# One-hot tables outside the sixth weight slot in a one-core MoE layer: the slot is loaded ahead of them, ScalarE scales their token half, and shared products run in another order

## The chip, the cores and the metric

The kernel runs on one core of one Trainium2 chip. The metric is the device time of one execution in microseconds (us). The profiled execution is a separate run whose span, from the first to the last instruction, is a little shorter than its own device time.

## What is computed

One layer of a hybrid decoder for 512 prompt tokens and 8 sample tokens (520 in all), width 1024, everything in float32. A token mixer (one input projection to seven parts, a short gated convolution, a Conformer convolution module, a gated merge and an output projection) is followed by a mixture of experts with 64 experts of width 256, of which each token takes 8, and one shared expert. The part that the change touches:

```python
m = sigmoid(g_a) * y_a + sigmoid(g_b) * y_b
x = x + gt1 * rmsnorm(m @ w_o, g_post1)
h = rmsnorm(x, g_pre2) * (1 + sc2) + sh2
scores = sigmoid(h @ w_router)             # 64 experts in 8 groups
# best 4 groups, then the 8 best experts of a token -> gate
act    = silu(h @ w1[e]) * (h @ w3[e]) * gate
routed = sum over e of act @ w2[e]
shared = (silu(h @ ws1) * (h @ ws3)) @ ws2
x = x + gt2 * rmsnorm(routed + shared, g_post2)
```

## The kernel before

Each engine has an instruction list written out by hand, and semaphores order the lists. An engine runs its own list strictly in order, so a wait holds up everything behind it. SP issues nearly all loads, ACT (ScalarE) issues the writes of small results, POOL (GpSimd) issues the gathers and scatters of token rows.

**The projection w_o.** Weights are split into a rounded part and a remainder, so that three fast products give the accuracy of float32. ACT makes the rounded part, POOL subtracts it from the loaded block in `raw` to get the remainder, 128 by 1024 elements at a time (L569 and L618). Items 72 to 79 are the eight column blocks of w_o, and their parts are kept in `w_kept`. TensorE (PE) uses them in `half_product(u)`, 24 matmuls for each u, once for tokens 0 to 255 and once for the others (L1746, L1747, L1750). The remainder of item 73 is written where the merged activations' remainder `m_lo` and others were needed before, so POOL waits at n = 73 until VectorE (DVE) has made the last piece of `m_lo` (L1247), and then serves items 73, 74 and so on. SP reloads a `raw` buffer once the remainder of its last item is there.

**Norm, residual, router.** After the sixteen half products PE, ACT and DVE alternate over x1, h2 and the router's logits. ACT copies x1 and h2, turned into token rows, out of PSUM and writes them to DRAM (`x1_dram`, semaphore `spill`; `h2_rows`, L1006 and L1008, semaphores `rows_out`). Token tile i has 128 tokens, and tile 4 has the last 8. DVE then picks the experts and gives every (token, expert) pair a place in a list of strips of 64 rows. There are at most 66 jobs of two strips (`JOBS`).

**The one-hot stage.** To turn places into row lists, DVE makes four arrays for each token tile: `oneEs` (job number equal, L1367, 528 half floats a partition), `oneA` (row number equal, L1368, 1024), and the two halves of `oneB`: `oneEs` times the token's number (L1370) and `oneEs` times the choice's number (L1371). PE multiplies them (L1856, 8 matmuls a tile, all summed in one bank). All five tiles' arrays lie side by side in the sixth weight slot, `act5[:, 2 * R + SLOT:...]`. PE then spreads the result (`idx_pe`, L1867), DVE makes the gather indices `idxG` (L1389), the run tables (`table_dve`) and a row of last passes (`early_dve` 1, L1408), and POOL issues the gather of pass 0 into `scr` and of pass 1 into `conv` (L645).

**The shared expert** is 16 + 16 + 32 matmuls of `shared_up(f, m, half)` (L1787) that PE runs wherever it would otherwise wait. ACT takes Silu (`shared_gate`) and a copy (`shared_value`), and POOL multiplies the two (`shared_gated`, L623).

**The expert loop.** Six weight slots of 3 MB each (w1, w3 and w2 of an expert). Experts 0 to 3 go to slots 1 to 4, expert 4 to slot 5 (the sixth), expert 5 to slot 0, and from expert 6 on a slot is refilled by SP (`refill`, L380 and L385) when PE has done its last pass with it. A pass takes two strips of 64 rows: DVE turns the gathered rows into `xe` (`rows_T`, L1444, two halves), PE makes the up products (L1882), DVE and ACT the activation, PE the down products (L1896), ACT copies out, and POOL scatters. The slots share memory with h2: the sixth lies where the one-hot arrays are and after them, `xe` lies over three of the eight blocks of `hT` that `shared_up` reads.

Of the kernel before, what the change touches and what calls it, by code (L numbers as in the profile page):

```python
# [7 lines left out]
F16 = mybir.dt.float16  # L8
I32 = mybir.dt.int32
U32 = mybir.dt.uint32  # L10
ALU = mybir.AluOpType
# [4 lines left out]
P = 128  # L16
# [6 lines left out]
def build_program(  # L23
# [33 lines left out]
    with ctx:  # L57
# [151 lines left out]
        one_of = act5[:, 2 * R + SLOT:2 * R + 2 * SLOT]  # L209
        NA, NB = TOPK * P // 2, TOPK * JOBS  # L210
        oneA = one_of[:, 0:TT * NA].bitcast(F16).rearrange("p (i k n r) -> p i k n r", i=TT, k=TOPK // 2, r=2)
        oneB = one_of[:, TT * NA:TT * (NA + NB)].bitcast(F16).rearrange("p (i k a n r) -> p i k a n r", i=TT, k=TOPK // 2, a=2, r=2)
        oneEs = [t.rearrange("p k e -> p (k e)")[:, 0:NB // 2].bitcast(F16).rearrange("p (k n r) -> p k n r", k=TOPK // 2, r=2) for t in (eq, eqm)]
        assert TT * (NA + NB) <= SLOT
# [18 lines left out]
        def s8(n):  # L233
# [47 lines left out]
                 "m_hi_dve aff_act gp_pe gm_dve early_dve early_pe last_pass_dve x1t_T x1t_done x1t_dve h2_dve oneE_dve sh_mm sh_ev sh_act "  # L281
# [49 lines left out]
        def _(sp):  # L331
# [56 lines left out]
            for k in range(3 * C):  # L388
                w = (w_out_a, w_out_b, w_o)[k // C]
                sp.wait_ge(S["w_lo"], 56 + k + (1 if k < 4 else 4))  # L390
# [4 lines left out]
            sp.wait_ge(S["w_lo"], 80 + NU)  # L395
# [12 lines left out]
            up_weights(1, 2, ((w1, 0),))  # L408
            sp.wait_ge(rows_out[0], 16 * 3)
# [4 lines left out]
            up_weights(4, 5)  # L414
            down_weights(4, 5)
# [94 lines left out]
        def _(pool):  # L510
# [102 lines left out]
            for n in range(72, 80):  # L613
                hi, lo = w_kept[n - 72]
                if n == 73:
                    pool.wait_ge(S["m_lo_dve"], C)
                pool.wait_ge(S["w_hi"], n + 1)
                pool.tensor_tensor(lo, raw[(n - 56) % 4], hi, ALU.subtract).then_inc(S["w_lo"], 1)  # L618
# [5 lines left out]

            shared_gated(0)
# [87 lines left out]
        def _(act):  # L713
# [283 lines left out]
            hx_at = [hx[:, 0, :], hx[:, 1, :], conv[:, 0:D], sflat[:, 0:D]]  # L997

            def h2_rows_out(i):
                n, t = (P if i < TT - 1 else LAST), hx_at[i % 4]  # L1000
                act.wait_ge(S["hx_T"], i + 1)
                if i == 2:
                    act.wait_ge(g2_out, 16)
                elif i == 4:
                    act.wait_ge(rows_out[0], 16 * 2)
# [23 lines left out]

            shared_value(0)  # L1030
            h2_rows_out(4)
            shared_gate(1)
# [42 lines left out]
        def _(dve):  # L1075
# [172 lines left out]

            dve.wait_ge(S["tailrows_act"], 1)
# [109 lines left out]
            def numbers(n):  # L1359
                return iot[:, 0:n, :].unsqueeze(1).to_broadcast([P, TOPK // 2, n, 2])  # L1360
# [4 lines left out]
            dve.wait_ge(spill, 16 * TT)  # L1365
            for i in range(TT):
                tt(oneEs[i % 2], numbers(JOBS), pairs_of(job_of[:, i], JOBS), ALU.is_equal).then_inc(S["oneE_dve"], 1)  # L1367
                tt(oneA[:, i], numbers(P), pairs_of(row_of[:, i], P), ALU.is_equal).then_inc(S["oneE_dve"], 1)  # L1368
                dve.wait_ge(S["oneE_dve"], 2 * i + 1)
                ts(oneB[:, i, :, 0], oneEs[i % 2], tokp1[:, i:i + 1], None, ALU.mult)  # L1370
                tt(oneB[:, i, :, 1], oneEs[i % 2], pairs_of(kv[:, i, :].rearrange("p (k r) -> p k r", r=2), JOBS), ALU.mult  # L1371
                   ).then_inc(S["idx_ab"], 1)
# [5 lines left out]
            dve.wait_ge(S["idx_mm"], 1)  # L1378
# [67 lines left out]

            dve.wait_ge(S["es_pe"], 2)
# [3 lines left out]
            dve.wait_ge(S["sh_mm"], 2 * FT)  # L1451
            for h in range(2):
                rows_T(0, 64, h)
# [53 lines left out]
        def _(pe):  # L1507
# [224 lines left out]
            def half_product(u):  # L1732

                a, b = part["AB"[u // C]]
                hi, lo = w_kept[item[u]]
                out = ps[:, u % 3, 0:b - a]
                if u < C:
                    pe.wait_ge(S["w_lo"], 72 + u + NU + 1)
# [12 lines left out]
                ins.then_inc(items_used, 1)  # L1751
# [28 lines left out]
            def shared_up(f, m, h, k0=0, k1=C):  # L1780
# [5 lines left out]
                for k in range(k0, k1):  # L1786
                    ins = mm(ps[:, bank, at:at + b - a], w[:, k, :], hT[:, k, a:b], start=(k == 0), stop=(k == C - 1))  # L1787
                if h == "B" and k1 == C:
                    ins.then_inc(S["sh_mm"], 1)

# [61 lines left out]
            shared_up(1, 0, "A")  # L1852
            for i in range(TT):
                pe.wait_ge(S["idx_ab"], i + 1)
                for k in range(TOPK):
                    ins = mm(ps[:, 7, 0:2 * JOBS], oneA[:, i, k // 2, :, k % 2],  # L1856
                             oneB[:, i, k // 2, :, :, k % 2].rearrange("p a n -> p (a n)"), start=(i == 0 and k == 0),
                             stop=(i == TT - 1 and k == TOPK - 1))
            ins.then_inc(S["idx_mm"], 1)
# [11 lines left out]
            shared_up(1, 1, "A")  # L1871
            pe.wait_ge(S["sh_ev"], 1)
            shared_up(1, 0, "B")
            pe.wait_ge(S["sh_ev"], 2)
            shared_up(1, 1, "B")
# [24 lines left out]
            pe.wait_ge(S["early_dve"], 1)  # L1900
            mm(ps[0:1, 6, P:P + 1 + TT], red[0:1 + TT, 2:3], ident[0:1 + TT, 0:1 + TT], start=True, stop=True).then_inc(S["es_pe"], 1)
# [140 lines left out]
```

## Time and profile before

| what | value |
|---|---|
| time, median of 3 runs | 1235.48 us (1234.01 to 1235.58) |
| the profiled execution's own time | 1235.82 us |
| its span | 1234.10 us |
| busy: PE, DVE, POOL, ACT | 95%, 46%, 42%, 26% |
| mean granted TensorE clock | 0.983 of full speed |
| read and written in DRAM | 322.21 MB and 33.30 MB |

How to read it: busy shares are taken over the whole span, and the stages differ. Up to about 500 us the projections run, to 557 us the w_o products, to 615 us norm, router, one-hot stage and the rest of the shared expert, and from there to 1196 us the expert loop. A granted clock of 1.00 is 2.4 GHz and 0.50 is 1.2 GHz.

### The profile page before, as it was taken

How to read it: one execution, taken by the hardware profiler on the slowest of the kernel's cores; microseconds unless marked ns; L12 is line 12 of the kernel's file. 1: busy time of each engine (PE TensorE's matmuls, PEld its weight loads, DVE VectorE, ACT ScalarE, POOL GpSimd, SP SyncE). 2: the span in 40 equal slices, each digit the busy share in tenths (PEclk: the TensorE clock that was granted, in tenths of full speed). 3: DMA queues.
4: the chain of work that ended last, by engine and by line, in shares of the span. 5: the costliest groups of instructions: out<-in, count | busy, mean ns of one | idle time of the engine just before them, and what ended most of it. 6: DMA issues, size and time to landing. Idle time of an engine off the chain costs nothing.

```text
span 1234.1 us, 26531 instructions
## 1 busy us (share of the span) xinstructions
PE 1167.9 (95%) x9397; PEld 847.9 (69%) x9398; DVE 563.0 (46%) x956; ACT 325.8 (26%) x633; POOL 514.3 (42%) x522
## 2 busy tenths in 40 slices
PE   4899999999999899999899999997989999899997
PEld 3599999999999899897755555544545554455542
DVE  4285676658568868337643322221112222222234
ACT  3522322323323451435121121111111111111122
POOL 2144444445448343600355444542344455344420
PEclk9899999999999899999999999998999999999999
DMA  9954345435421233548399999999999999999887
GB/s 307 324 177 147 86 146 166 140 91 160 151 81 41 69 85 101 143 168 338 127 405 410 401 397 412 411 414 415 413 411 413 411 413 399 411 415 410 342 319 267
DMA packets 149035, 337.48 MB, mean 273 GB/s; under 512 B 14807, under 2 KB 99363, under 8 KB 123369
## 3 DMA queue, kind: packets, MB, share of 16 engines
q1 hardware_dynamic: 129304, 296.57, 64.0%
q0 software_dynamic: 16656, 34.14, 7.3%
q10 hardware_dynamic: 3025, 6.07, 1.4%
q8 instruction: 35, 0.57, 0.2%
q14 instruction: 15, 0.12, 0.0%
HBM read 322.21 MB, written 33.30 MB: 288 GB/s over the span
## 4 chain that ended last, share of the span: by engine, by line
PE 74%; DMA 13%; issue 5%; DVE 4%; POOL 2%; SPq 1%; ACT 0%; DVEq 0%; POOLq 0%; ACTq 0%
PE ps L1882 23%; DMA w<-in_w_dram 10%; PE ps L1896 10%; PE ps L1602 9%; PE ps L1603 9%; PE ps L1604 9%; DMA ring<-in_w_ada_dram 2%; PE ps L1890 2%; PE ps L1746 1%; PE ps L1955 1%; PE ps L1615 1%; PE ps L1747 1%; PE ps L1750 1%; PE ps L1988 1%; PE ps L1544 1%
## 5 line engine op out<-in xcount | busy, mean ns | idle before, releaser
L1882 PE MATMUL ps<-w,xe 128*64 (+1 forms) x3136 | 378.2, 393 | 21.1 <-DMA w<-in_w_dram 19.2
L1882 PEld LDWEIGHTS ps<-w,xe 128*64 128x64 f32 x3136 | 221.6, 136 | 171.7 <-issue 55.8
L569 POOL TENSOR_TENSOR wsplit<-ring,wsplit 128x1024 fp32r<-128x1024 f32 x72 | 175.3, 2435 | 252.2 <-ACT wsplit L721 222.1
L1602 PE MATMUL ps<-h_s_hi,wsplit 128*128 128x260 f32 x960 | 272.3, 284 | 0.0
L1604 PE MATMUL ps<-h_s_hi,wsplit 128*128 128x260 f32 x960 | 270.8, 282 | 0.0
L1603 PE MATMUL ps<-h_lo_m_hi,wsplit 128*128 128x260 f32 x832 | 234.9, 282 | 0.0
L1464 DVE TENSOR_TENSOR rs<-sg,ps 128x128 f32<-128x128 f32 x98 | 28.2, 288 | 365.5 <-ACT sg L1051 365.5
L1602 PEld LDWEIGHTS ps<-h_s_hi,wsplit 128*128 128x128 f32 x960 | 180.8, 188 | 6.7 <-issue 5.9
L1896 PE MATMUL ps<-w,eactT 128*64 128x512 f32 (+1 forms) x784 | 184.8, 592 | 0.0
L1604 PEld LDWEIGHTS ps<-h_s_hi,wsplit 128*128 128x128 f32 x960 | 180.9, 188 | 0.0
L1603 PEld LDWEIGHTS ps<-h_lo_m_hi,wsplit 128*128 128x128 f32 x832 | 156.7, 188 | 0.0
L1164 DVE SCALAR_TENSOR_TENSOR ps<-conv,vecs,ps 128x512 f32<-128x512 f32 x224 | 154.7, 746 | 0.0
L721 ACT ACTIVATE wsplit<-ring 128x1024 fp32r<-128x1024 f32 x74 | 78.5, 1061 | 274.0 <-PE ps L1604 267.3
L645 POOL DMA_INDIRECT scr<-h_rows,gidx x100 | 102.1, 1021 | 42.8 <-issue 22.9
L645 POOL DMA_INDIRECT conv<-h_rows,gidx x100 | 101.3, 1013 | 44.4 <-issue 24.6
L1896 PEld LDWEIGHTS ps<-w,eactT 128*64 128x64 f32 x784 | 54.3, 136 | 64.4 <-issue 53.6
L640 POOL COPY gidx<-tail 128x4 int32 (+1 forms) x50 | 10.5, 210 | 188.3 <-DVE xe L1444 180.0
L1039 ACT ACTIVATE act<-ps 128x1024 f32<-128x1024 f32 x50 | 51.2, 1024 | 117.5 <-PE ps L1896 112.6
L1051 ACT ACTIVATE sg<-ps 128x128 f32<-128x128 f32 x98 | 27.1, 277 | 190.8 <-PE ps L1882 190.8
L1053 ACT ACTIVATE eactT<-ps 128x128 f32<-128x128 f32 x98 | 27.2, 277 | 172.2 <-PE ps L1890 172.2
L1444 DVE STREAM_TRANSPOSE xe<-conv 128x512 f32<-128x512 f32 x50 | 56.2, 1123 | 33.8 <-PE ps L1882 30.2
L1444 DVE STREAM_TRANSPOSE xe<-scr 128x512 f32<-128x512 f32 x50 | 55.9, 1119 | 31.3 <-PE ps L1882 31.3
(357 smaller groups left out, 1373.0 us busy)
## 6 DMA issues: line engine op xcount, KB each, us to landing
w<-in_w_dram SPq DMA_DIRECT2D x192, 1024.0 KB, 21.6
ring<-in_w_in_dram SPq DMA_DIRECT2D x56, 512.0 KB, 3.8
ring<-in_w_ada_dram SPq DMA_DIRECT2D x8, 2048.0 KB, 8.8
ring<-in_w_ada_dram SPq DMA_DIRECT2D x8, 1024.0 KB, 26.5
ring<-y_rows SPq DMA_DIRECT2D x4, 2048.0 KB, 18.2
ring<-in_w_out_a_dram SPq DMA_DIRECT2D x8, 512.0 KB, 3.6
ring<-in_w_out_b_dram SPq DMA_DIRECT2D x8, 512.0 KB, 3.5
ring<-in_w_o_dram SPq DMA_DIRECT2D x8, 512.0 KB, 3.7
```

The costliest lines, as they stand in the source:

```text
L569: pool.tensor_tensor(wsplit[:, b, 1], raw[raw_slot], wsplit[:, b, 0], ALU.subtract).then_inc(S["w_lo"], 1)
L645: pool.indirect_dma_start(out=xgs[u][:, g * QR:(g + 1) * QR], out_offset=None, in_=h2_rows.rearrange("t (q d) -> (t q) d", q=4), in_offset ...
L721: act.activation(wsplit[:, b, 0], raw[raw_slot], ACT.Copy).then_inc(S["w_hi"], 1)
L1039: act.activation(yb[:, 1 - u, :], ps[:, 4:6, :].rearrange("p b n -> p (b n)"), ACT.Copy).then_inc(S["ex_yd"], 1)
L1164: chain(stt(out=acc[k % 2] if k != KC - 2 else cvj, in0=glu[:, k:k + NP], scalar=vecs[:, ds(j + (V_WC + 8 * k), 1)], in1=acc[k % 2], op0=A ...
L1444: dve.transpose(out=xe[:, 4 * h:4 * h + 4, :].rearrange("p k (g s) -> p g k s", g=4), in_=xgs[u].rearrange("p (g r k) -> p g k r", g=4, k= ...
L1464: tt(eact[:, cols], esil[:, cols], ps[:, 2 + f, P:2 * P], ALU.mult).then_inc(S["ex_mul"], 1)
L1602: mm(ps[:, bank + h, 0:HT], wsplit[:, b, 0, k, :], hi[:, k, p:q], start=(k == 0), stop=False)
L1603: mm(ps[:, bank + h, 0:HT], wsplit[:, b, 0, k, :], lo[:, k, p:q], start=False, stop=False)
L1604: ins = mm(ps[:, bank + h, 0:HT], wsplit[:, b, 1, k, :], hi[:, k, p:q], start=False, stop=(k == C - 1))
L1882: ins = mm(ps[a * STRIP:(a + 1) * STRIP, 2 + f, 0:2 * P], xe[:, k, a * STRIP:(a + 1) * STRIP], w[a][:, f, k], start=(k == 0), stop=(k == C ...
L1896: ins = mm(ps[a * STRIP:(a + 1) * STRIP, 4 + h, :], eactT[:, k, a * STRIP:(a + 1) * STRIP], w[a][:, k, h * 512:(h + 1) * 512], start=(k == ...
```

## The change

1. **Item 73.** DVE, right after the last piece of `m_lo`, subtracts item 73 itself. POOL skips it and waits for DVE before item 74. PE's second half product waits for DVE. SP's block k = 21 waits for DVE too, and the other counts of `w_lo` go down by one.
2. **One-hot buffers.** The arrays of tile i lie in one of two buffers, in `conv` and in `scr`. DVE and ACT wait for PE's use of a buffer two tiles back. The h2 rows of tiles 2 and 3, which lay there, go through the two `hx` buffers, with waits for the writes of two tiles back.
3. **The sixth slot.** Expert 4 is loaded by SP as soon as the x1 rows are written. It was loaded after the one-hot products and the first gather.
4. **Token half.** ACT makes the token half of `oneB` for each tile (`token(i)`), in its list between the h2 copies and around `shared_value(0)`.
5. **Shared products.** `shared_up(1, 0, "A")` is cut into four pairs of steps between the tiles' products. The first three steps of the remaining three products (those that read what `xe` covers) come first, then the small product L1901 that follows `early_dve` 1, then the other fifteen steps. DVE's first `rows_T` waits for the nine steps only and stands ahead of the table step for `early_dve` 2, for which PE waits before it enters the expert loop.
6. **POOL** waits for the last one-hot product before `shared_gated(0)`.

```diff
+        ones_at = [conv[:, 0:NA + NB], sflat[:, 0:NA + NB]]
...
-            sp.wait_ge(S["idx_mm"], 1)
-            sp.wait_ge(xg_in[0], 64)
+            sp.wait_ge(spill, 16 * TT)
             up_weights(4, 5)
             down_weights(4, 5)
+            sp.wait_ge(rows_out[0], 16 * 3)
+            sp.wait_ge(rows_out[1], 16 * 2)
+            down_weights(5, 0)
...
+            pool.wait_ge(S["idx_mm"], TT)
             shared_gated(0)
...
+            def token(i):
+
+                act.wait_ge(S["oneE_dve"], 2 * i + 1)
+                if i >= 2:
+                    act.wait_ge(S["idx_mm"], i - 1)
+                act.activation(oneB[i % 2][:, :, 0], oneEs[i % 2], ACT.Copy, scale=tokp1[:, i:i + 1]).then_inc(S["token_act"], 1)
+
+            token(0)
+            token(1)
             shared_value(0)
             h2_rows_out(4)
+            for i in range(2, TT):
+                token(i)
...
+            dve.wait_ge(S["w_hi"], 74)
+            tt(w_kept[1][1], raw[1], w_kept[1][0], ALU.subtract).then_inc(S["m_lo_dve"], 1)
...
             for i in range(TT):
+                if i >= 2:
+                    dve.wait_ge(S["token_act"], i - 1)
                 tt(oneEs[i % 2], numbers(JOBS), ...)
+                if i >= 2:
+                    dve.wait_ge(S["idx_mm"], i - 1)
+                tt(oneA[i % 2], numbers(P), ...)
-                ts(oneB[:, i, :, 0], oneEs[i % 2], tokp1[:, i:i + 1], None, ALU.mult)
+                tt(oneB[i % 2][:, :, 1], oneEs[i % 2], ...).then_inc(S["idx_ab"], 1)
...
+            dve.wait_ge(S["h2_read"], 1)
+            for h in range(2):
+                rows_T(0, 64, h)
             dve.wait_ge(S["es_pe"], 2)
             link(ts(last_pass, ps[0:1, 6, P:P + 1 + TT], 4.0 * P - 1.0, None, ALU.add), "early_dve")
...
+                ins.then_inc(S["idx_mm"], 1)
+                if i < TT - 1:
+                    shared_up(1, 0, "A", 2 * i, 2 * i + 2)
...
+            turn = (1, 2, 3, 0, 4, 5, 6, 7)
+            shared_up(1, 1, "A", 0, 3, turn)
+            pe.wait_ge(S["sh_ev"], 2)
+            shared_up(1, 0, "B", 0, 3, turn)
+            shared_up(1, 1, "B", 0, 3, turn).then_inc(S["h2_read"], 1)
+            pe.wait_ge(S["early_dve"], 1)
+            mm(ps[0:1, 6, P:P + 1 + TT], ...).then_inc(S["es_pe"], 1)
+            shared_up(1, 1, "A", 3, C, turn)
+            shared_up(1, 0, "B", 3, C, turn)
+            shared_up(1, 1, "B", 3, C, turn)
```

## Rows read from the trace of the kernel before

**Rows 1.** Waits of PE from 600 us on: total us, times, longest us.

```profile
PE ps L1882 <- DMA w<-in_w_dram: 19.2, 6, 6.2
PE ps L1856 <- DVE act L1371: 1.1, 2, 0.9
```

**Rows 2.** Timeline of PE: start, duration, line, tiles, count, idle before.

```profile
603.21 10.84 PE L1787 MATMUL ps<-act,ring 128*128 128x256 f32 x48
...
615.92 6.57 PE L1882 MATMUL ps<-w,xe 128*64 x56 [1.76 <-DVE xe L1444]
...
627.58 6.51 PE L1882 MATMUL ps<-w,xe 128*64 x56
...
638.76 6.53 PE L1882 MATMUL ps<-w,xe 128*64 x56
```

**Rows 3.** Windows: each engine's busy time, then granted clock, DMA share, GB/s.

```profile
586.00:588.00 2.00, 2.00 (x28) 1.68 (x26) 1.00 (x6) 0.36 (x2) 0.00 (x0) 1.00 0.23 88
...
616.00:618.00 2.00, 2.00 (x18) 1.31 (x20) 2.00 (x2) 0.00 (x0) 1.98 (x3) 1.00 0.99 414
...
700.00:705.00 5.00, 5.00 (x42) 2.37 (x40) 3.34 (x5) 0.83 (x3) 1.42 (x2) 1.00 0.86 329
...
760.00:780.00 20.00, 20.00 (x164) 11.21 (x162) 4.17 (x6) 3.71 (x8) 10.94 (x14) 1.00 1.02 415
```

**Rows 4.** Timeline around item 73.

```profile
502.23 2.41 POOL L618 TENSOR_TENSOR wsplit<-ring,wsplit 128x1024 fp32r<-128x1024 f32 x1 [5.71 <-DVE m_lo L1247]
502.47 2.26 DVE L1252 SCALAR_TENSOR_TENSOR s<-ada,vecs 128x72 f32<-128x72 f32 x1
...
504.69 0.39 PE L1746 MATMUL ps<-h_lo_m_hi,wsplit 128*128 128x256 f32 x1 [2.10 <-POOL wsplit L618]
```

**Rows 5.** A window of 1 us, and two steps of the chain that ended last.

```profile
506.00:507.00 1.00, 1.00 (x7) 1.00 (x6) 0.00 (x0) 0.00 (x0) 1.00 (x2) 0.50 0.86 259
...
509.58 0.32 PE ps L1746
...
512.86 0.32 PE ps L1746
```

**Rows 6.** Groups of DVE by form: count, then total us and mean ns.

```profile
L1504 DVE TENSOR_TENSOR act<-act,ring 128x1024 f32<-128x1024 f32 x4 | 4.9, 1225 | 0.1
```

**Rows 7.** Timeline of DVE in the one-hot stage, tiles 0 and 1.

```profile
592.51 0.43 DVE L1367 TENSOR_TENSOR act<-iot,act 128x528 f16<-128x528 f16 x1
...
593.47 0.35 DVE L1370 TENSOR_SCALAR act<-act,tokp 128x528 f16<-128x528 f16 x1
...
595.02 1.38 DVE L1370 TENSOR_SCALAR act<-act,tokp 128x528 f16<-128x528 f16 x1
```

**Rows 8.** Timeline of PE in the one-hot stage.

```profile
594.64 3.62 PE L1787 MATMUL ps<-act,ring 128*128 128x256 f32 x16
598.10 1.59 PE L1856 MATMUL ps<-act 128*128 128x132 f16 x24
```

**Rows 9.** Timeline of ACT and POOL in the one-hot stage.

```profile
594.25 0.39 ACT L1022 ACTIVATE rs<-ps 128x264 f32<-128x264 f32 x1
...
594.71 1.54 POOL L623 TENSOR_TENSOR scr<-sg,rs 128x520 f32<-128x520 f32 x1 [71.94 <-ACT rs L1022]
594.84 1.01 ACT L1006 ACTIVATE ring<-ps 8x1024 f32<-8x1024 f32 x1 [0.21 <-PE ps L1831]
```

**Rows 10.** Timeline of DVE from the index products to pass 1.

```profile
602.51 0.17 DVE L1382 TENSOR_SCALAR table<-act 1x64 int32<-1x64 f32 x1
...
603.44 0.69 DVE L1389 TENSOR_SCALAR tail<-ps,red 128x264 int32<-128x264 f32 x1
...
614.52 2.07 DVE L1444 STREAM_TRANSPOSE xe<-scr 128x512 f32<-128x512 f32 x2
```

**Rows 11.** Timeline of SP's queue: the loads of expert 4's w1 and w3.

```profile
612.66 0.80 SPq L380 DMA_DIRECT2D w<-in_w_dram  x2
```

**Rows 12.** The chain of work that ended last, a step at 847 us.

```profile
847.29 0.50 issue
```

More of the change, by code:

```diff
@@ L208, in build_program @@
         sflat = scr[:, :, :].rearrange("p n t -> p (n t)")
-        one_of = act5[:, 2 * R + SLOT:2 * R + 2 * SLOT]
         NA, NB = TOPK * P // 2, TOPK * JOBS
-        oneA = one_of[:, 0:TT * NA].bitcast(F16).rearrange("p (i k n r) -> p i k n r", i=TT, k=TOPK // 2, r=2)
-        oneB = one_of[:, TT * NA:TT * (NA + NB)].bitcast(F16).rearrange("p (i k a n r) -> p i k a n r", i=TT, k=TOPK // 2, a=2, r=2)
+        ones_at = [conv[:, 0:NA + NB], sflat[:, 0:NA + NB]]
+        assert NA + NB <= min(sum(wide_n), 4 * T)
+        oneA = [t[:, 0:NA].bitcast(F16).rearrange("p (k n r) -> p k n r", k=TOPK // 2, r=2) for t in ones_at]
+        oneB = [t[:, NA:NA + NB].bitcast(F16).rearrange("p (k a n r) -> p k a n r", k=TOPK // 2, a=2, r=2) for t in ones_at]
         oneEs = [t.rearrange("p k e -> p (k e)")[:, 0:NB // 2].bitcast(F16).rearrange("p (k n r) -> p k n r", k=TOPK // 2, r=2) for t in (eq, eqm)]
-        assert TT * (NA + NB) <= SLOT
         QR = D // 4
@@ L408, in _ @@
             up_weights(1, 2, ((w1, 0),))
+            sp.wait_ge(spill, 16 * TT)
+            up_weights(4, 5)
+            down_weights(4, 5)
             sp.wait_ge(rows_out[0], 16 * 3)
@@ L615, in _ @@
                 if n == 73:
-                    pool.wait_ge(S["m_lo_dve"], C)
+                    continue
+                if n == 74:
+                    pool.wait_ge(S["m_lo_dve"], C + 1)
                 pool.wait_ge(S["w_hi"], n + 1)
@@ L1778, in logits, with shared_up @@
                 mark(ins, "logits_pe")
-            def shared_up(f, m, h, k0=0, k1=C):
+            def shared_up(f, m, h, k0=0, k1=C, turn=tuple(range(C))):
                 w = ws13[:, m].rearrange("p (k n) -> p k n", k=C)[:, :, f * P:(f + 1) * P]
@@ L1785, in shared_up @@
                 bank = 3 - 3 * f if h == "A" else 1 + m
-                for k in range(k0, k1):
-                    ins = mm(ps[:, bank, at:at + b - a], w[:, k, :], hT[:, k, a:b], start=(k == 0), stop=(k == C - 1))
+                for n in range(k0, k1):
+                    k = turn[n]
+                    ins = mm(ps[:, bank, at:at + b - a], w[:, k, :], hT[:, k, a:b], start=(n == 0), stop=(n == C - 1))
                 if h == "B" and k1 == C:
                     ins.then_inc(S["sh_mm"], 1)
+                return ins
             pe.wait_ge(S["t_cp"], 16)
@@ L1851, in _ @@
             h2_T(4)
-            shared_up(1, 0, "A")
             for i in range(TT):
                 pe.wait_ge(S["idx_ab"], i + 1)
+                pe.wait_ge(S["token_act"], i + 1)
                 for k in range(TOPK):
-                    ins = mm(ps[:, 7, 0:2 * JOBS], oneA[:, i, k // 2, :, k % 2],
-                             oneB[:, i, k // 2, :, :, k % 2].rearrange("p a n -> p (a n)"), start=(i == 0 and k == 0),
+                    ins = mm(ps[:, 7, 0:2 * JOBS], oneA[i % 2][:, k // 2, :, k % 2],
+                             oneB[i % 2][:, k // 2, :, :, k % 2].rearrange("p a n -> p (a n)"), start=(i == 0 and k == 0),
                              stop=(i == TT - 1 and k == TOPK - 1))
-            ins.then_inc(S["idx_mm"], 1)
+                ins.then_inc(S["idx_mm"], 1)
+                if i < TT - 1:
+                    shared_up(1, 0, "A", 2 * i, 2 * i + 2)
             pe.wait_ge(S["es_dve"], 1)
@@ L1869, in _ @@
             mark(ins, "idx_pe")
-            shared_up(1, 1, "A")
-            pe.wait_ge(S["sh_ev"], 1)
-            shared_up(1, 0, "B")
+            turn = (1, 2, 3, 0, 4, 5, 6, 7)
+            assert R + D >= R + T and R + 2 * D <= R + 4 * T
+            shared_up(1, 1, "A", 0, 3, turn)
             pe.wait_ge(S["sh_ev"], 2)
-            shared_up(1, 1, "B")
+            shared_up(1, 0, "B", 0, 3, turn)
+            shared_up(1, 1, "B", 0, 3, turn).then_inc(S["h2_read"], 1)
+            pe.wait_ge(S["early_dve"], 1)
+            mm(ps[0:1, 6, P:P + 1 + TT], red[0:1 + TT, 2:3], ident[0:1 + TT, 0:1 + TT], start=True, stop=True).then_inc(S["es_pe"], 1)
+            shared_up(1, 1, "A", 3, C, turn)
+            shared_up(1, 0, "B", 3, C, turn)
+            shared_up(1, 1, "B", 3, C, turn)
             pe.wait_ge(S["sh_ev"], 3)
```

39 lines of the change are left out of this document (17 added, 22 removed).

## The prediction, on record before the changed kernel ran

> **What bounds the kernel now.** I read the page first: PE is busy 95% of the span and DMA is near its ceiling in the second half, so both are candidates there. The waits of PE from 600 us on come next [rows 1]: 19.2 us in six waits for expert weights, and 1.1 us for the one-hot arrays. The timeline of PE gives the pace of the loop [rows 2]: passes 1 and 2 start at 627.58 and 638.76, so a pass without a stall takes 11.18 us, and pass 0 took 11.66. Windows tell who leads [rows 3]. In 760 to 780 the DMA engines are full (share 1.02, 415 GB/s). In 700 to 705 the share is 0.86: 0.7 us in which nothing was left to transfer. At that moment every free slot had been refilled, and the next load waited for PE to free one. This one row decides what the early load of expert 4 is worth. Before it PE never stalls, after it every load is asked for when PE frees a slot. So the end of the kernel moves with PE's passes at 700 us, which is with the start of the loop.
>
> The start of the loop is set by a chain of waits: the subtraction of item 73 (PE idle 2.10 us before 504.69 [rows 4]), the half products, the router, DVE's one-hot arrays, the index, the first gather, `rows_T`, and PE at 615.92 after 1.76 us idle [rows 2].
>
> **The change part by part.** Times are on the clock of before, and each part is taken as if the ones ahead of it had not shifted it.
>
> *Item 73.* POOL starts at 502.23, right when DVE finishes `m_lo`, takes 2.41 us, and PE starts at 504.69 [rows 4]. DVE does the same subtraction right behind `m_lo`, with no hop. Its cost is not in the trace at this place. The row of the same size, float32, two inputs in SBUF, 1024 elements, is 1.225 us [rows 6]. PE starts 2.41 - 1.23 = 1.2 us earlier, at 503.5. Queued behind it on DVE are three small operations that nobody waits for (`fold2`, `ada`, `s1`). In exchange they no longer stand under POOL: L1252, 72 elements, took 2.26 us [rows 4]. POOL's items 74 and 75 follow at 503.4 and end near 505.8 and 508.2. PE needs them at about 506.8 and 510, so no new stall. SP's block 21 is issued 1.2 us earlier. Gain 1.2 us.
>
> *The clock behind it.* After this idle time the granted clock was 0.50 in 506 to 507, and the level at 1.00 is the usual one. The third half product starts at 509.58 and the fourth at 512.86 [rows 5], so one takes 3.28 us. The second, from 504.69 to 509.58, took 4.89, so the fall cost 1.6 us. With DVE's version the second idle piece is 0.9 us in place of 2.10. The idle time of 1.76 us before 615.92 was not followed by a fall (616 to 618: 1.00 [rows 2, 3]). So I take it that the clock stays. Bounds 0 and 1.6 us, taken 1.6.
>
> *One-hot stage.* DVE now makes three arrays a tile. L1367 and L1368 take 593.47 - 592.51 = 0.96 us and L1371, as large as L1367, at most 0.43, so 1.4 us a tile. Before, tile 1's L1370 began 595.02 - 593.47 = 1.55 us after tile 0's [rows 7]. Also, tile 1's L1370 took 1.38 in place of 0.35 us while POOL's `shared_gated(0)` ran (594.71, 1.54 us [rows 9]). That meeting is gone. DVE would be done nearly 2 us earlier, but PE then sets the end. From 594.64 PE has 3.62 us of shared steps (16 records, 8 steps) and five tiles at 1.59 / 3 = 0.53 us [rows 8]: 594.64 + 3.62 + 2.65 = 600.9, or 601.0 with hops. Before, the same work had 1.1 us of waiting for L1371 in it [rows 1] and ended near 602.1. Gain up to 1.1 us.
>
> Does ACT keep up? Its cost for 528 half floats is not in the trace. By its rows for 264 and 1024 elements, 0.39 and 1.01 us, it lies between these, on the line at 0.6 [rows 9]. Tokens 0 and 1 end near 593.6 and 594.8. Then come `shared_value(0)` (0.67), `h2_rows_out(4)` (1.01, to 596.4), its DMA issue (0.3) and token 2, done near 597.4. PE wants it at 597.55. The margin is 0.1 us and what waits behind is the index. I take 0.3 us off: 0.8 us of gain in the index.
>
> *POOL moved behind the last one-hot product.* `shared_gated(0)` now takes up to 1.54 us [rows 9] from just behind the last product, exactly when DVE makes the index. Behind the copy of `tok1` come six small operations, of which L1382 is the first that reads SBUF [rows 10]. Nothing in the trace shows such an operation under POOL. Nearest is L1370, also a tensor_scalar with one SBUF input, which POOL held for 1.03 us [rows 7]. L1382 started 0.4 us after the last product, so POOL could hold it for some 1.54 - 0.4 = 1.1 us. Bounds 0 and 1.1 us on `idxG` and on the gather, taken 1.0. The Trainium skill says on its page "SBUF — State Buffer", section "Who interferes with whom", that a tensor_scalar or copy from SBUF to SBUF can take the port pair that VectorE shares with GpSimd, and that whoever starts first then blocks the other for its whole length. L1370 agrees with 1.38 us against 0.35. By the page the sum below stands, and if small operations escaped the rule it would be 1.0 us more.
>
> *Gather, `rows_T`, the door of the loop.* The first gather had landed by 612.66, where SP went on [rows 11]. `idxG` moves by 0.8 - 1.0, which is 0.2 us later, so the gather lands at 612.8. Before, `rows_T` waited for the last shared step (PE until 614.05 [rows 2]) and began at 614.52. Now it begins at the landing and takes 2.07 us [rows 10], to 614.9. Then comes the table step (0.15), and PE waits for that before it enters the loop. The entry was hidden and now is not: in the chain at 847 us it is 0.50 us of issue [rows 12]. PE starts at 615.5 in place of 615.92: gain 0.4 us. PE itself is ready at 614.05 - 0.8 = 613.25, which is not the last. With the index unblocked the start is 614.5, a gain of 1.4.
>
> *Pass 0* took 11.66 us, because the gather of pass 1 landed late, with 5 MB of weights issued at 612.66 and 614.08 [rows 11]. Now 3 MB of these are gone and the pass takes 11.2: gain 0.5 us.
>
> *Expert 4's loads* (three DMAs of 1 MB) pass expert 5's w2 on SP and share the engines with four row writes of ACT's queue. They free 3.15 MB at 415 GB/s = 7.6 us of DMA time behind 612.66. Between 615 and 700 nobody waits for DMA, and at 700 the lead is gone: worth 0.
>
> **Sum.** 1.2 + 1.6 + 0.4 + 0.5 = 3.7 us. The profiled execution took 1235.82 (span 1234.10, 1.72 around it), 0.34 above the median. It becomes 1232.1, and the median 1231.8.
>
> **The rivals.**
> - *The clock falls all the same* (0.15). About 1.9 us without work are left around 503 (0.9 and the piece ahead of it), hardly different from the 1.76 us that went without a fall, and one row is thin evidence. Gain 2.1 us: 1233.4.
> - *The writes of h2 hold ACT* (0.15). `h2_rows_out(4)` waits for the write of tile 2. The earlier traffic ends by about 586 (586 to 588: share 0.23 [rows 3]). From there expert 4 takes 7.6 us and three row tiles of 0.5 MB 1.3 us each, so everything has landed by 597.5 in any order. ACT wants it at 595.5. Token 2 and the index come up to 2.0 us later: gain 1.7, 1233.8. Speaking against it: the write is issued at about 589 and shares, so it need not be last.
> - *DMA leads after all* (0.12). If the 0.7 us at 700 [rows 3] are only a gap between two requests while a queue stands, the 7.6 us count in full where PE waits for weights (19.2 us [rows 1]): 1227.9.
> - *Slower* (0.08). The ring DVE, ACT, PE over two buffers is paced by ACT's `token`. Tokens 2, 3 and 4 are on the path one after the other. To end 2.5 us above before, they must eat 3.7 + 2.5 = 6.2 us, so each has to take 0.6 + 2.1 = 2.7 us, 4 times the line through ACT's rows. No row excludes it, since none shows ACT writing half floats with a stride: say 3.0 us each, 1235.5 - 3.7 + 7.2 = 1239.0. Under 1.8 us each it stays faster than before.
>
> **The numbers.** 0.2% of 1235.48 is 2.5 us, about what a measurement of this kernel can tell from no change: faster is under 1233.0, slower over 1238.0. The forecast case has 0.50, with its own range 1230.8 (index unblocked, 4.7 us) to 1233.0 (token 2 late by some 1.2 us). I put 0.03 of it past the bound. Faster 0.47 + 0.12, same 0.03 + 0.30, slower 0.08: 0.59, 0.33, 0.08. The range leaves out the slow case and the DMA case, 0.20 together. Its low end is 1230.8 less the 1.5 us by which runs of before differ, 1229.3, and its high end is both middle rivals together, 3.7 - 1.6 - 2.0 = 0.1, which is 1235.4.
>
> **What would show it.** PE's second half product starts 1.2 us sooner after DVE's `m_lo`, with clock 1.00 behind it. The six small DVE operations before L1389 have a gap as long as POOL's L623. PE has no idle time over 0.3 us between the one-hot tiles. PE enters the loop about 0.6 us after the second `rows_T`. The DMA share falls under 0.9 in parts of 640 to 700 and is full again from 720 on. PE's waits for weights stay near 19 us. Wrong would be: these waits fall by several us (DMA led), or token 2 ends after PE's second pair of shared steps (ACT leads), or the clock row shows 0.50 near 504.

## The result, and the profile after

The changed kernel is slower, by 0.24%: 1239.97 us (median of 6 runs, 1237.68 to 1240.44) against 1235.05 of the kernel before on the same chip (6 runs), a ratio of 1.0024 with a 95% interval of 1.0014 to 1.0035. The forecast was 1231.8. The profiled execution took 1239.92 us, its span is 1237.8 and its mean granted clock 0.979. So 2.1 us of its time lie outside the span, where the kernel before has 1.7. That holds in every run on record: 2.0 to 2.2 us in all versions in which ACT makes the token half, 1.7 to 1.9 in the kernel before and in the two versions without it (item 73 alone, token half by DVE). No trace shows what these 0.4 us are, and no table of stages below contains them.

Cutting the region of the change at events that every version has shows where the time went. "One-hot" runs from DVE's first one-hot operation to where PE starts what follows its last index product, "to loop" from there to PE's first expert product. Then come pass 0 (to the first product of pass 1) and the rest of the span.

| profiled execution, us | first one-hot op at | one-hot | to loop | pass 0 | rest |
|---|---|---|---|---|---|
| before | 592.51 | 9.71 | 13.70 | 11.66 | 606.5 |
| after | 589.86 | 12.57 | 14.89 | 12.82 | 607.7 |
| after less before | -2.65 | +2.86 | +1.19 | +1.16 | +1.2 |

The differences add up to +3.76, which is the difference of the spans (+3.7). The first item is close to the 2.8 us promised for item 73. The three behind it were forecast as -0.8, +0.4 and -0.5. The last is not a property of the change: over the 14 profiled executions of this case the rest lies between 605.7 and 608.2 us, more of it goes with more waiting of PE for weights (17.7 to 21.8 us), and the changed kernel itself had 607.7 once and 606.0 once (below).

Item 73 and the clock behind it, in the timeline and a window of after (windows as in [rows 3]); they answer to [rows 4, 5]:

```profile
502.31 1.22 DVE L1263 TENSOR_TENSOR wsplit<-ring,wsplit 128x1024 fp32r<-128x1024 f32 x1
...
503.58 0.38 PE L1766 MATMUL ps<-h_lo_m_hi,wsplit 128*128 128x256 f32 x1 [0.75 <-DVE wsplit L1263]
504.00:506.00 2.00, 2.00 (x19) 2.00 (x18) 2.00 (x1) 0.67 (x2) 2.00 (x1) 1.00 0.57 173
```

1.22 us in place of 2.41, PE starts at 503.58 in place of 504.69, and the clock stays at 1.00.

The chain that ended last, through the one-hot stage of after (start, duration, piece; short steps between these are left out):

```profile
585.65 0.93 ACT ring L1008
...
586.60 8.43 DMA h_rows<-ring
...
595.11 1.02 ACT ring L1008
...
596.55 0.74 ACT conv L1037
...
597.43 0.80 PE ps L1878 x8
```

Read it upwards. PE's product for tile 2 waited for ACT's `token(2)` (L1037). That stood in ACT's list behind `h2_rows_out(4)` (L1008). That waited for the h2 row write of tile 2, which ACT had begun to issue at 586.60 and which landed 8.43 us later. The timeline of ACT and PE at the same place, which answers to [rows 8, 9]:

```profile
595.11 1.01 ACT L1008 ACTIVATE ring<-ps 8x1024 f32<-8x1024 f32 x1 [2.21 <-DMA h_rows<-ring]
596.55 0.73 ACT L1037 ACTIVATE conv<-act,tokp 128x528 f16<-128x528 f16 x1 [0.42 <-ACT ring L1008]
597.43 0.80 PE L1878 MATMUL ps<-conv 128*128 128x132 f16 x8 [2.50 <-ACT conv L1037]
```

ACT stood 2.21 us. PE takes its list in order, so it stood too, for 2.50 us. Behind this idle time the granted clock is at the lower level (0.50), and again behind the entry to the loop. The windows of after, one from each place:

```profile
598.00:600.00 2.00, 2.00 (x9) 1.46 (x7) 1.66 (x7) 0.73 (x1) 0.00 (x0) 0.50 0.49 86
618.00:620.00 2.00, 2.00 (x12) 1.17 (x10) 1.79 (x2) 0.00 (x0) 1.85 (x2) 0.56 1.02 427
```

The windows of 2 us from 596 to 602 have a mean clock of 0.94, 0.50 and 0.71, those from 618 to 622 one of 0.56 and 0.59. If the clock has the two levels 1.00 and 0.50, that is 3.4 us at the lower one each time. 3.4 us at half clock hold 1.7 us of full-speed work, so each fall costs up to 1.7 us. From the index to the loop, DVE, ACT and PE of after ([rows 2, 10]):

```profile
602.88 1.03 DVE L1400 TENSOR_SCALAR table<-act 1x64 int32<-1x64 f32 x1
604.57 0.69 DVE L1407 TENSOR_SCALAR tail<-ps,red 128x264 int32<-128x264 f32 x1
613.86 2.08 DVE L1462 STREAM_TRANSPOSE xe<-scr 128x512 f32<-128x512 f32 x2 [6.08 <-DMA scr<-h_rows,gidx]
615.15 0.39 ACT L1024 ACTIVATE rs<-ps 128x264 f32<-128x264 f32 x1
615.86 0.11 DVE L1470 TENSOR_SCALAR table<-ps 1x6 int32<-1x6 f32 x1
617.32 8.17 PE L1912 MATMUL ps<-w,xe 128*64 x56 [2.49 <-issue]
...
630.14 6.51 PE L1912 MATMUL ps<-w,xe 128*64 x56
```

The 64-element L1400 took 1.03 us under POOL's `shared_gated(0)`, against 0.17 before. The table step ends at 615.97, and PE's first product comes 1.35 us later. In pass 0 the same 56 products take 8.17 us, in pass 1 6.51: that is the half clock, 1.6 us of it.

### The profile page after: what moved, and what is told of

The parts are those of the page before. It is cut to its first block, busy times and chain, and to the rows that moved or that the text cites. A ratio compares the mean times of both kernels' runs of the same rounds, so it can differ in the third digit from the quotient of the medians.

```text
span 1237.8 us, 26539 instructions
## 1 busy us (share of the span) xinstructions
PE 1171.0 (95%) x9397; PEld 849.9 (69%) x9398; DVE 562.5 (45%) x952; ACT 329.6 (27%) x638; POOL 512.4 (41%) x521
## 4 chain that ended last, share of the span: by engine, by line
PE 75%; DMA 14%; issue 5%; DVE 3%; POOL 1%; SPq 1%; ACT 1%; DVEq 0%; POOLq 0%; ACTq 0%
PE ps L1912 24%; DMA w<-in_w_dram 10%; PE ps L1926 10%; PE ps L1620 9%; PE ps L1621 9%; PE ps L1622 9%; DMA ring<-in_w_ada_dram 2%; PE ps L1920 2%; PE ps L1983 1%; PE ps L1633 1%; PE ps L1766 1%; PE ps L1767 1%; PE ps L1770 1%; PE ps L2016 1%; PE ps L1808 1%
## 5 line engine op out<-in xcount | busy, mean ns | idle before, releaser
L1926 PE MATMUL ps<-w,eactT 128*64 (+1 forms) x784 | 184.8, 592 | 0.0
```

Source lines behind the costliest of these rows:

```text
L1926: ins = mm(ps[a * STRIP:(a + 1) * STRIP, 4 + h, :], eactT[:, k, a * STRIP:(a + 1) * STRIP], w[a][:, k, h * 512:(h + 1) * 512], start=(k == ...
```

## The experiments

Each ratio is to the kernel before on the same chip, with its 95% interval, from 9 to 12 runs of each kernel and 17 to 31 of before. The line numbers in rows are those of the kernel they are from.

### Item 73 alone

The kernel before, with nothing but part 1 of the change. The core of the edit:

```diff
+            dve.wait_ge(S["w_hi"], 74)
+            tt(w_kept[1][1], raw[1], w_kept[1][0], ALU.subtract).then_inc(S["m_lo_dve"], 1)
```

> The kernel before with the subtraction of item 73 on VectorE alone. Theory 1 (this part saves 1.2 us of work and 1.4 to 1.6 us of half clock, and all of it reaches the end): the one-hot stage starts 2.7 us sooner and the time is 1232.4, 2.7 us below before. Rival (what is won ahead of the expert loop is lost again by waits for weights in the loop, because loads are asked for at the same times): 1234.5 or more, with more than 21 us of waits for weights.

Measured: 1233.53 us, 0.9975 (0.9965 to 0.9985), about 3.1 us faster; the prediction had 2.8 for this part. The granted clock is 1.00 from 504 to 508, the first expert product starts at 613.80 in place of 615.92, and PE's waits for weights are 19.1 us, so nothing is lost again there: the rival is out. It is the part of the change that worked. The other five parts together therefore turn 0.9975 into 1.0024, some 6 us, and these are what the next runs divide.

### Expert 4's load late again

```diff
-            sp.wait_ge(spill, 16 * TT)
-            up_weights(4, 5)
-            down_weights(4, 5)
...
             down_weights(5, 0)
+            sp.wait_ge(S["idx_mm"], TT)
+            sp.wait_ge(xg_in[0], 64)
+            up_weights(4, 5)
+            down_weights(4, 5)
```

> The changed kernel with expert 4 loaded where it was before, behind the index and the first gather. Theory 1 (the early load holds the row write of tile 2, and with it the tokens of tiles 2 and 3 on ScalarE): the 2.2 us of waiting of h2_rows_out(4) and the 2.5 us of PE ahead of the tile 2 products go, so does the half clock behind them, and the index ends about 3.9 us sooner; the late entry to the loop (2.5 us idle, then half clock) stays. Time 1235 to 1236, 3.5 to 4 us under the changed kernel. Rival (the tokens are slow by themselves, or the row write is slow without the load too): PE still stands over 2 us in the one-hot stage and the time stays within 1 us of the changed kernel.

Measured: 1234.34 us, 0.9981 (0.9972 to 0.9990). PE's idle time ahead of the third tile's product falls from 2.50 to 0.16 us, and the last h2 rows go out without a wait. Timeline:

```profile
592.47 1.00 ACT L1009 ACTIVATE ring<-ps 8x1024 f32<-8x1024 f32 x1
...
594.77 0.64 PE L1879 MATMUL ps<-conv 128*128 128x132 f16 x8 [0.16 <-ACT conv L1038]
...
613.02 6.57 PE L1913 MATMUL ps<-w,xe 128*64 x56 [2.49 <-issue]
```

The view of the tile `h_rows` gives the time from the issue of a row write to its landing. First after, then this kernel:

```profile
DMA to landing us min/median/max: 3.3/5.5/7.8
```

```profile
DMA to landing us min/median/max: 2.7/2.9/3.2
```

So with the early load under way the row writes of 0.5 MB land up to 4.6 us later. The last line of the timeline matters too: PE enters the loop here after the same 2.49 us of idle time as in after, and the 56 products take 6.57 us, at full clock. That was not expected, and it is why the run gives back 5.3 us and not the 3.5 to 4 written down: 4.0 in the one-hot stage (8.59 in place of 12.57) and 1.6 in pass 0 (11.23 in place of 12.82).

### The last h2 rows behind the tokens in ACT's list

```diff
-            h2_rows_out(4)
             for i in range(2, TT):
                 token(i)
+            h2_rows_out(4)
```

> The changed kernel with the copy of the last h2 tile behind the tokens of tiles 2 to 4 in ScalarE's list; the load of expert 4 stays early. Theory 1 (the position in ScalarE's in-order list is what turns the late write into a wait of PE): PE's idle time in the one-hot stage falls from 2.5 us to under 0.5, the half clock there goes, the index ends 3.5 to 4 us sooner, time 3.5 to 4 us under the changed kernel, 1235 to 1236. Rival (the early load slows the stage in another way, or the last rows written later now hold the gather): less than 1.5 us gained.

Measured: 1233.86 us, 0.9977 (0.9966 to 0.9988). Expert 4's load stays early and its writes land just as late (up to 7.8 us), but nothing that PE needs stands behind them. Timeline:

```profile
595.47 0.64 PE L1878 MATMUL ps<-conv 128*128 128x132 f16 x8
596.21 0.74 ACT L1037 ACTIVATE conv<-act,tokp 128x528 f16<-128x528 f16 x1 [0.58 <-DVE act L1384]
596.85 1.00 ACT L1008 ACTIVATE ring<-ps 8x1024 f32<-8x1024 f32 x1
...
613.53 6.57 PE L1912 MATMUL ps<-w,xe 128*64 x56 [2.30 <-issue]
```

The one-hot stage takes 8.27 us and pass 0 11.30, against 12.57 and 12.82. One line moved in one list gives back 5.8 us of the 1240 by the ratios. Expected were 3.5 to 4; the surplus is again pass 0.

### The token half by DVE again

```diff
+                ts(oneB[i % 2][:, :, 0], oneEs[i % 2], tokp1[:, i:i + 1], None, ALU.mult)
```

`token(i)` and its waits are left out.

> The changed kernel with the token half made by VectorE again, the early load left in. Theory 1 (the late row write costs only because the tokens stand behind it in ScalarE's list): h2_rows_out(4) still waits over 2 us but PE does not wait for it in the one-hot stage; idle there under 0.6 us, ratio 0.998. Rival (the tokens are needed on ScalarE because VectorE is then last): VectorE's five arrays take 1.6 us each and PE waits 1 us or more in total, ratio 0.999 to 1.000.

Measured: 1234.11 us, 0.9983 (0.9975 to 0.9992). ACT still stands for the row write, even longer, as the chain of waits and the timeline say, but PE's product for tile 2 starts before ACT is through:

```profile
ACT ring L1008 <- DMA h_rows<-ring: 3.1, 1, 3.1
```

```profile
596.96 0.64 PE L1872 MATMUL ps<-conv 128*128 128x132 f16 x8
...
597.28 1.01 ACT L1008 ACTIVATE ring<-ps 8x1024 f32<-8x1024 f32 x1 [3.12 <-DMA h_rows<-ring]
```

The three runs cut the same chain at its three links (the load that makes the write late, the place in the list behind the write, the engine that PE's operand comes from). Each gives back 5 to 6 us, by its ratio against that of after (1.0024 and, measured again, 1.0025). In each both falls of the clock behind 590 us are gone.

### The table step ahead of `rows_T` again

```diff
-            dve.wait_ge(S["h2_read"], 1)
-            for h in range(2):
-                rows_T(0, 64, h)
             dve.wait_ge(S["es_pe"], 2)
             link(ts(last_pass, ps[0:1, 6, P:P + 1 + TT], 4.0 * P - 1.0, None, ALU.add), "early_dve")
+            dve.wait_ge(S["h2_read"], 1)
+            for h in range(2):
+                rows_T(0, 64, h)
```

> The changed kernel with VectorE's table step for the last passes ahead of rows_T again, as before, so that PE can enter the expert loop while VectorE still waits for the gather. Theory 1 (the entry costs PE some 1.3 us after that step and is now exposed, and the 2.5 us of idle time behind it bring the half clock): PE starts pass 0 about 1.5 us sooner relative to the landing of the first gather, 0.3 us after the first rows_T half, the half clock in pass 0 goes with it (1.6 us), time about 3 us under the changed kernel, 1237. Rival (the entry is bound by the gather and the transposes whatever the order): less than 0.7 us gained.

Measured: 1237.99 us, 1.0014 (1.0003 to 1.0025); its interval overlaps that of after, so the gain of 3 us that was expected is not shown. The profile is clearer. The one-hot stage is as bad as in after (12.69), the way to the loop is 0.6 us shorter (14.28) and pass 0 1.1 us shorter (11.69). Timeline:

```profile
597.16 0.80 PE L1878 MATMUL ps<-conv 128*128 128x132 f16 x8 [2.62 <-ACT conv L1037]
...
614.89 0.38 ACT L1024 ACTIVATE rs<-ps 128x264 f32<-128x264 f32 x1
616.44 6.58 PE L1912 MATMUL ps<-w,xe 128*64 x56 [1.87 <-DVE xe L1462]
```

ACT's last copy of shared products ends at 615.27 and PE starts 1.17 us later. In the kernel before, the same copy ended at 614.76 and PE started at 615.92, 1.16 us later:

```profile
614.37 0.39 ACT L1022 ACTIVATE rs<-ps 128x264 f32<-128x264 f32 x1
```

So with the table step off the path the copy sets the entry. It had already been a limit in the kernel before. It was not alone there: the first half of `rows_T` ended near 615.6 (two in 2.07 us from 614.52), 0.3 us ahead of PE's start, and the profile names it as what came last. The clock fell in the one-hot stage here too, but not behind this shorter wait of 1.87 us.

### Both repairs, and three more steps from there

Both repairs (last rows moved, table step ahead) in one kernel; then each of the next three by itself on top of it: POOL no longer waits for the last one-hot product; `shared_gated(0)` stands between the first two gathers; expert 4 is late as well (the edit of the load shown further up). The first of the three is the edit shown here.

```diff
-            pool.wait_ge(S["idx_mm"], TT)
             shared_gated(0)
```

> The changed kernel with both repairs: the last h2 copy behind the tokens, and the table step ahead of rows_T. Theory 1 (two separate losses, each with its half clock): they add, index at about -3.9 us and entry 0.6 us sooner than with the first repair alone; the loop starts 3.5 to 4 us sooner than before and the ratio to the kernel before is 0.997 (1232 to 1233). Rival (one bound behind both: the loop cannot start sooner than the gather lets it, or DMA gives it back): no better than with the first repair alone, 0.9977.

> The same with GpSimd's shared_gated(0) at its old place, without the wait for the last one-hot product. Theory 1 (GpSimd held VectorE's small SBUF operations for 1.0 us on the way to the gather indices, and the gather to rows_T to entry chain is last): the gap of L1400 (1.03 us) goes and moves to an array of the one-hot stage where PE is last, so the gather lands 1.0 us sooner. If the entry is bound by ScalarE's last copy of the shared products and the loop entry (1.2 us) and not by the gather, the time changes by less than 0.3 us; if by the gather, it falls 1 us.

> The two repairs with shared_gated(0) between GpSimd's gathers of pass 0 and pass 1. Theory 1: neither the one-hot arrays nor the index operations meet it, the gather of pass 0 is issued 1.0 us sooner; the loop starts sooner by that only as far as the gather is last, so 0 to 1 us under the kernel with both repairs. Rival: the gather of pass 1 is 1.3 us later and pass 0 ends with a wait, 0 to 1 us over it.

> The two repairs with expert 4 loaded late again. Theory 1 (the 7.6 us of DMA lead are gone by 700 us, because the slots are refilled at PE's pace): within 0.5 us of the kernel with both repairs and the early load. Rival (DMA leads in the loop and the early load is worth its transfer): 3 to 7 us slower than with the early load, and more waits for weights than 20 us.

| kernel | median us | ratio (95%) | one-hot | to loop | pass 0 | rest |
|---|---|---|---|---|---|---|
| both repairs | 1233.41 | 0.9986 (0.9977 to 0.9995) | 8.27 | 14.29 | 11.81 | 605.7 |
| and no wait on POOL | 1232.67 | 0.9976 (0.9967 to 0.9985) | 8.43 | 14.15 | 11.23 | 607.3 |
| and POOL between gathers | 1233.03 | 0.9976 (0.9967 to 0.9985) | 8.28 | 14.21 | 12.12 | 606.0 |
| and expert 4 late | 1232.76 | 0.9979 (0.9969 to 0.9989) | 8.27 | 14.34 | 11.97 | 606.1 |

No two of the intervals are apart, nor is the first from that of the one-line repair (0.9977): that the two repairs add up is not shown. Three things can be read.

First, without POOL's wait the long hold is on a one-hot operation of 1024 elements, not on the index. DVE and POOL of that kernel:

```profile
592.06 2.33 POOL L627 TENSOR_TENSOR scr<-sg,rs 128x520 f32<-128x520 f32 x1 [72.85 <-ACT rs L1023]
...
593.16 1.78 DVE L1386 TENSOR_TENSOR scr<-iot,act 128x1024 f16<-128x1024 f16 x1
...
597.77 0.17 DVE L1399 TENSOR_SCALAR table<-act 1x64 int32<-1x64 f32 x1
```

There DVE has slack (the stage is 0.16 us longer), and the index gets its 0.17 back. Yet the way to the loop shrinks by only 0.14 us. PE's first product comes 1.20 us behind the end of ACT's copy there (610.33 and 611.53) and 1.18 with both repairs, so the copy sets the entry in both.

Second, the early load's lead is real and is spent before it is worth anything. Windows of the kernel with both repairs, then of the one whose load is late as well:

```profile
640.00:645.00 5.00, 5.00 (x44) 2.69 (x41) 2.57 (x5) 0.83 (x3) 1.31 (x3) 1.00 0.81 297
695.00:700.00 5.00, 5.00 (x48) 2.95 (x44) 1.99 (x4) 0.83 (x3) 1.93 (x3) 1.00 0.93 365
```

```profile
640.00:645.00 5.00, 5.00 (x40) 2.49 (x38) 3.00 (x7) 0.83 (x3) 1.22 (x3) 1.00 0.98 372
695.00:700.00 5.00, 5.00 (x44) 2.77 (x42) 2.75 (x4) 0.83 (x3) 1.14 (x2) 1.00 0.91 344
```

At 640 one has room on its DMA engines (0.81 against 0.98), at 695 both have the same (0.93 and 0.91), and the rest behind pass 0 is 605.7 and 606.1 us. PE waits 17.8 and 18.9 us for weights. The DMA rival, 3 to 7 us in favour of the early load, is out; a difference under 1 us could hide in the intervals.

Third, pass 0 takes 11.8 to 12.1 us in three of the four and 11.23 in the one without the wait. The last DMA of pass 1's gather is issued there 0.58 us before the loop starts, and 0.08 to 0.70 behind its start in the others. Timelines with both repairs, then without the wait:

```profile
612.55 6.58 PE L1912 MATMUL ps<-w,xe 128*64 x56 [1.87 <-DVE xe L1462]
612.69 1.00 POOL L650 DMA_INDIRECT conv<-h_rows,gidx  x1 [0.31 <-issue]
...
620.18 1.11 DVE L1462 STREAM_TRANSPOSE xe<-conv 128x512 f32<-128x512 f32 x1 [2.04 <-DMA conv<-h_rows,gidx]
```

```profile
610.95 1.00 POOL L649 DMA_INDIRECT conv<-h_rows,gidx  x1 [0.30 <-issue]
611.53 6.58 PE L1911 MATMUL ps<-w,xe 128*64 x56 [1.91 <-issue]
...
618.42 1.13 DVE L1461 STREAM_TRANSPOSE xe<-conv 128x512 f32<-128x512 f32 x1 [2.00 <-DMA conv<-h_rows,gidx]
```

DVE gets the rows of pass 1 7.63 us after the loop's start in the one and 6.89 in the other. With POOL's product between the gathers this DMA is issued 0.70 us behind the start, and pass 0 is longest (12.12). So by these stages the index hold of 1.03 us has a price after all, 0.14 us on the way to the loop and 0.58 in pass 0, but only once the loop starts early enough for the second gather to be late. That this price reaches the end is not shown: both spans are 1230.1 us, and the intervals overlap.

### The wait for ACT's copy inside the loop

The version without POOL's wait, with PE's wait for the copy moved from ahead of the loop to just before the first up product.

```diff
-            pe.wait_ge(S["sh_ev"], 4)
...
+                        pe.wait_ge(S["sh_ev"], 4)
```

> Both repairs, GpSimd's old place, and PE's wait for ScalarE's last copy (sh_ev 4) moved from ahead of the loop into it, just before the first product. Theory 1 (PE needs 1.2 us from that copy to the first product because the loop's entry stands behind it): the entry runs while ScalarE copies, the first product starts 0.3 us after the later of that copy and rows_T's first half, so 0.5 to 0.9 us sooner than with the wait ahead; ratio to before 0.997. Rival (one more wait in each of the 49 passes costs more than this, or the gather is last): no gain or a loss of up to 1 us.

Measured: 1232.61 us, 0.9972 (0.9962 to 0.9982), the lowest ratio of all, though not apart from that of the same kernel with the wait ahead (0.9976). Timeline:

```profile
611.12 0.39 ACT L1023 ACTIVATE rs<-ps 128x264 f32<-128x264 f32 x1
...
612.33 2.48 PE L1911 MATMUL ps<-w,xe 128*64 x20 [1.53 <-ACT rs L1023]
```

From the end of the copy to the first product it is 0.82 us, in place of 1.20; 0.3 was expected. So 0.4 us of the entry went under the wait. What the other 0.82 are is not shown: the way from the semaphore to the product, or what was left of the entry, since PE's own last shared product had ended only at 610.8. To the loop takes 13.78, 0.37 less. In the time this is not resolved.

### Expert 4 early, but behind the row writes

```diff
             sp.wait_ge(spill, 16 * TT)
-            up_weights(4, 5)
-            down_weights(4, 5)
             sp.wait_ge(rows_out[0], 16 * 3)
             sp.wait_ge(rows_out[1], 16 * 2)
             down_weights(5, 0)
+            up_weights(4, 5)
+            down_weights(4, 5)
```

> The changed kernel with expert 4's load just behind the last h2 row write and expert 5's w2, some 16 us earlier than in the kernel before but behind the writes. Theory 1 (only the meeting of the load with the row writes does harm, not that it is early): the wait of h2_rows_out(4) and PE's 2.5 us in the one-hot stage go as with the late load, ratio 0.998. Rival (the load slows the one-hot stage or the gather in another way): ratio over 1.000.

Measured: 1235.98 us, 0.9997 (0.9989 to 1.0006): no better than the kernel before. The interval of the late load (0.9972 to 0.9990) just touches this one. The writes land in 3.0 us at most and the one-hot stage takes 8.59, as with the late load, but the loads now meet the first gather. The DMA share is 1.00 to 1.02 from 600 to 608, where it is 0.00 to 0.28 with the late load, and DVE waits longer for the rows (6.1 us with the late load):

```profile
DVE xe L1462 <- DMA scr<-h_rows,gidx: 6.9, 1, 6.9
```

To the loop it takes 15.69 us, 0.8 more than with the late load. The rest of the difference is not accounted for by this place. Its profiled execution also had half clock near 504, as others have had (below).

### The changed kernel once more

> The changed kernel itself once more, since the experiments were each timed against the kernel before on other occasions. If the loss is a property of the kernel and its repairs are worth what they seem: ratio 1.002 to 1.004, h2_rows_out(4) waits 2 to 3 us for the row write, PE stands 2.5 us in the one-hot stage. If the first result was an accident of a few runs: ratio under 1.000.

Measured: 1238.66 us (12 runs) against 1235.41 (17 of before), 1.0025 (1.0015 to 1.0035). Its stages are 12.42, 14.77 and 12.83 us, with 2.4 us of idle time ahead of the loop and half clock in the windows from 596 to 602 (0.93, 0.50, 0.72) and from 618 to 622 (0.55, 0.60). These repeat. The rest is 606.0 against 607.7, and PE's waits for weights are 17.7 against 20.0 us, so the +1.2 of the first table belongs to that execution and not to the change.

## Why the prediction was wrong, step by step

- **Item 73, right.** Forecast 1.2 and, for the clock, 1.6; measured 1.1 between the starts of PE, 2.65 at the first one-hot operation (which lies between 588.7 and 590.3 in all executions whose clock holds near 504), and 3.1 us by the run of this part alone. One aside was wrong without harm: the small operations behind it do still stand under POOL, now under item 74 (the one of 72 elements took 2.31 us in the run of this part alone). The rival that the clock falls all the same is seen in 3 of 13 profiled executions with this edit (last rows behind the tokens alone, load behind the writes, token half by DVE), so its chance of 0.15 was fair. In after itself it did not come.
- **"Does ACT keep up?", the step that failed.** It gave token 2 a margin of 0.1 us and took 0.3 off. ACT's operation itself was no problem (0.73 us against 0.6). What stood ahead of it in ACT's list was: `h2_rows_out(4)` waits for the write of tile 2, and this is the rival "the writes of h2 hold ACT", which got 0.15. Its wait of up to 2.0 us was right (2.21). What spoke against it, that a write which shares need not be last, was wrong: begun at 586.60, it landed 8.4 us later by the chain, at 595.03, which is 597.7 on the clock of before and so as late as the rival's bound of 597.5. And its price was too low by half, since half clock followed the idle time that it gives to PE. Against the repaired kernels (8.3 to 8.7, take 8.4) the stage of after lost 2.50 us of waiting and up to 1.7 us by the 3.4 us of half clock, together 4.2, and 8.4 + 4.2 = 12.6 stands against 12.57 measured.
- **POOL behind the last one-hot product, right.** Forecast 1.0 us on the index; the row says 1.03 in place of 0.17, so 0.9 later. "SBUF — State Buffer" of the Trainium skill, section "Who interferes with whom", held for an operation of 64 elements as well: this one from SBUF to SBUF, begun 0.3 us behind POOL's product, ended when that one did. But it was not on the path by its full length: in the repaired kernel its removal shortens the way to the loop by 0.14 us and pass 0 by 0.58.
- **"The entry was hidden and now is not: 0.50 us", wrong in both halves.** 0.50 was the price at a pass inside the loop. The first entry takes 1.35 us behind the table step, 1.17 behind ACT's copy. And it was not hidden before: from the end of that copy at 614.76 to PE's start it is 1.16 us, which is what the copy to the first product takes where the copy alone sets the entry (1.17 to 1.23), so an earlier `rows_T` would have gained nothing. "PE itself is ready at 613.25, which is not the last" left that copy out. Forecast +0.4 us for the whole stretch from the index products to the loop; measured +1.2.
- **Pass 0, wrong in sign.** Forecast -0.5, measured +1.2, all of it and more by the second 3.4 us of half clock: 12.82 less 1.6 is the 11.2 forecast, which the kernels with late load, moved rows or token half by DVE show (11.23, 11.30, 11.29). That the clock would stay was taken from one row with 1.76 us idle; here it was 2.49. What makes it fall is not settled. After 2.49, 2.30, 2.41 and 3.28 us ahead of the loop in the kernels with late load, moved rows, token half by DVE and load behind the writes it stayed at 1.00. It fell in both executions of after (2.49 and 2.37 us), where the one-hot stage had already held one fall. With that earlier fall and 1.87 us of idle time (table step ahead) it stayed.
- **Expert 4's lead worth 0, right.** PE's waits for weights are 20.0 us, 19.2 before, and the pair with both repairs and early or late load does not differ (0.9986 and 0.9979). "DMA leads after all" is out. What the step missed is that the transfer has a price where it runs: it meets either the row writes or the first gather.
- **"Slower", near in number and wrong in cause.** The rival with a chance of 0.08 had 1239.0 us, and its bound of 1238.0 was passed. But it took ACT's tokens for slow, at 3.0 us each; they take 0.73. That it came near is luck.

The sum then reads, against the forecast: 0.15 us less at item 73, 3.7 us worse in the one-hot stage, 0.8 on the way to the loop, 1.7 in pass 0, and 1.2 of that execution's own. That is 7.5 us, from the forecast of -3.7 to the +3.76 of the first table. The profiled time moved by 4.1: the forecast kept 1.72 us around the span, and it was 2.1.

Open: whether anything but item 73 gains. Alone it has 0.9975, and the best version of all the parts 0.9972. The repaired kernels win 1.1 to 1.4 us in the one-hot stage by the profile. Against that, the one with both repairs stands 0.6 us longer on the way to the loop (14.29 and 13.70), 0.15 in pass 0, and 0.4 outside the span, which leaves about 0.3.

## What to carry to other kernels

A transfer brought forward isn't free because nobody waits for it: look up which small transfers run at that time and what stands in order behind their landing, and put nothing urgent behind such a wait in an engine's list. Where a wait gives TensorE over 2 us with no work, count the half clock as a risk on top of its price: in the one-hot stage it followed all three times (2.33 to 2.62 us idle), and 2.5 us cost 4.2, while ahead of the loop it followed 2 of 6 such waits (2.30 to 3.28 us). Before pricing a step as hidden or shown, find what sets the end now, the last small copy included. And run the parts of a change alone: here one of six gave as much as any version of all of them, within what the runs can tell.

## What the runs showed that was not expected

- A write of 0.5 MB from ACT's queue landed in 2.6 to 3.2 us with expert 4's load late, and in up to 7.8 us (8.7 in one run) beside its three loads of 1 MB from SP's queue.
- The first entry to the expert loop took TensorE 1.16 to 1.35 us from the last step that it waited for ahead of the loop to the first product, and 0.82 when that wait stood inside.
- The same idle time ahead of the same products, 2.49 us, was followed by a granted clock of 0.56 in 618 to 620 in one kernel, and by full-speed products (6.57 us for 56) in another.
- Time outside the span was 1.7 to 1.9 us in versions without ACT's tokens and 2.0 to 2.2 in those with them, in every run.
